# The compare that makes the one-hots of a gate matrix: its row of column numbers read from a PSUM bank

## The reference, cut to what matters

```python
s1, i1 = lax.top_k(s[:, :, 0], P_TOPK)
s2, i2 = lax.top_k(s[:, :, 1], P_TOPK)
cand_i = (i1[..., :, None] * P_NKEYS + i2[..., None, :]).reshape(nt, P_HEADS, P_TOPK * P_TOPK)
top_s, pos = lax.top_k(cand_s, P_TOPK)
idx = jnp.take_along_axis(cand_i, pos, axis=-1)
gate = jax.nn.softmax(top_s, axis=-1)
u = jnp.take(u_tab, idx, axis=0)
act = jax.nn.gelu(jnp.einsum('thkd,td->thk', u, xb), approximate=False) * gate
vv = jnp.take(v_tab, idx, axis=0)
return jnp.einsum('thk,thkd->td', act, vv)
```

## Time and profile before

| | us |
|---|---|
| median of 3 runs | 4235.46 |
| lowest, highest | 4233.41, 4239.32 |
| profiled execution | 4235.86 |
| its span, first to last instruction | 4234.1 |
| busy in the span: PE, DVE, ACT, POOL | 3680.3, 3221.9, 1264.6, 2074.4 |
| gate matrix stage of the first layer, first compare to last evacuation | 1047.0 to 1203.7 |
| of the second layer | 2956.9 to 3113.3 |

### The profile page before, as it was taken

The page is one execution under the profiler, slowest core; times in us unless marked ns, Lnnn a source line. Parts: engine busy times, 40 slices in busy tenths (PEclk is TensorE's granted clock), DMA queues, the critical chain, the costliest instruction groups (busy, mean ns, idle before and its releaser), DMA issues. The chain is left out here.

```text
span 4234.1 us, 51468 instructions
## 1 busy us (share of the span) xinstructions
PE 3680.3 (87%) x17523; PEld 2894.4 (68%) x17523; DVE 3221.9 (76%) x5977; ACT 1264.6 (30%) x2010; POOL 2074.4 (49%) x1349
## 2 busy tenths in 40 slices
PE   6985579896779999999997957894779999999997
PEld 2454355443669989988986546452668998998996
DVE  1036554577979999999998167298979999999998
ACT  1031131111743333333332133101743333333332
POOL 0000000134967767777875000034966777778775
PEclk8987689898989999999998955997989999999999
DMA  4410001341579999999997100111569999999997
GB/s 199 163 43 6 0 1 40 130 170 51 159 233 396 396 398 400 391 405 401 398 397 307 67 23 1 50 40 40 158 221 394 397 398 399 398 401 402 398 396 304
DMA packets 318724, 1013.09 MB, mean 239 GB/s; under 512 B 23351, under 2 KB 121655, under 8 KB 296089
## 3 DMA queue, kind: packets, MB, share of 16 engines
q0 software_dynamic: 149936, 546.03, 33.1%
q1 hardware_dynamic: 166882, 440.55, 27.5%
q10 hardware_dynamic: 1800, 25.24, 1.6%
HBM read 958.16 MB, written 53.56 MB: 239 GB/s over the span
## 5 line engine op out<-in xcount | busy, mean ns | idle before, releaser
L1331 POOL DMA_INDIRECT arena<-in_peer_v,picked x512 | 834.1, 1629 | 238.5 <-issue 122.5
L1331 POOL DMA_INDIRECT arena<-in_peer_u_rows,picked x512 | 765.2, 1495 | 346.5 <-DVE dots L1924 220.4
L831 PE MATMUL pair<-h_hi,u_hi 128*128 128x384 f32 x2048 | 689.5, 337 | 30.9 <-issue 30.9
L831 PE MATMUL pair<-h_lo,u_hi 128*128 128x384 f32 x2048 | 687.5, 336 | 0.0
L831 PE MATMUL pair<-h_hi,u_lo 128*128 128x384 f32 x2048 | 687.2, 336 | 0.0
L1944 DVE SCALAR_TENSOR_TENSOR gate<-arena,act,gate 128x1024 f32<-128x1024 f32 x512 | 640.7, 1279 | 6.7 <-DVE act L1936 6.6
L1924 DVE CUSTOM_DVE_ANT_0 arena<-arena 128x1024 f32<-128x1024 f32 x512 | 612.3, 1219 | 15.1 <-DVE dots L1930 15.1
L831 PEld LDWEIGHTS pair<-h_hi,u_hi 128*128 128x128 f32 x2048 | 387.5, 189 | 40.0 <-issue 34.3
L1108 ACT ACTIVATE u_hi<-ring 128x2048 fp32r<-128x2048 f32 x128 | 245.5, 1919 | 519.5 <-DMA ring<-in_peer_u 519.4
L831 PEld LDWEIGHTS pair<-h_lo,u_hi 128*128 128x128 f32 x2048 | 387.4, 189 | 6.4
L831 PEld LDWEIGHTS pair<-h_hi,u_lo 128*128 128x128 f32 x2048 | 387.1, 189 | 0.0
(11 more groups left out here) (300 smaller groups left out, 5810.5 us busy)
## 6 DMA issues: line engine op xcount, KB each, us to landing
ring<-in_peer_u SPq DMA_DIRECT2D x128, 1024.0 KB, 8.0
ring<-in_peer_v SPq DMA_DIRECT2D x128, 1024.0 KB, 9.3
routing<-arena SPq DMA_DIRECT2D x24, 2048.0 KB, 8.7
arena<-routing SPq DMA_DIRECT2D x64, 768.0 KB, 9.8
ring<-in_w_ada SPq DMA_DIRECT2D x12, 2048.0 KB, 10.2
ring<-in_w_ada ACTq DMA_DIRECT2D x12, 2048.0 KB, 7.8
ring<-in_peer_wq SPq DMA_DIRECT2D x8, 2048.0 KB, 7.9
ring<-in_w_in SPq DMA_DIRECT2D x6, 2048.0 KB, 12.9
```

The lines of the kernel that those rows point to most:

```text
L831: last = mm(pair[:, j, 0:TD], R(u[b][:, P * (KD * j + k):P * (KD * j + k + 1)]), R(h[:, k, :]), start=(k == 0 and i == 0), stop=(k == KD - ...
L1331: pool.indirect_dma_start(gathered[:, b, :], None, rows, bass.IndirectOffsetOnAxis(picked[:, n:n + 1], 0)).then_inc(sem[f"row_in{b}"], 16)
```

## The change

At the beginning of DVE's `routing_matrix` a copy puts the 128 column numbers into the first 128 words of `bank[1]` in PSUM, and waits for its end. The compare of every job reads them from there. Nothing else differs.

```diff
             def routing_matrix(l):
+                link(V.tensor_copy(bank[1][:, 0:P], iota))
                 jobs = TB // 4
...
                             dve.wait_ge(sem["g_full"], i * (2 * jobs) + (hot0 + m + 1))
                             tt(hots[:, m % 4], bc(cols[:, b, 0:2, 4 * n:4 * n + 4], P, 3),
-                               bc(bc(iota, 4, 1), 2, 1), ALU.is_equal).then_inc(sem["hot_ready"], 1)
+                               bc(bc(bank[1][:, 0:P], 4, 1), 2, 1), ALU.is_equal).then_inc(sem["hot_ready"], 1)
```

## The result

| | before | after |
|---|---|---|
| median of 4 runs, us | 4237.14 | 4168.23 |
| lowest, highest | 4233.41, 4239.32 | 4165.0, 4170.4 |
| profiled execution, its span | 4235.9, 4234.1 | 4165.0, 4163.2 |

The changed kernel is faster: the ratio of the times is 0.984, with a 95% interval of 0.9826 to 0.9854. That is 68.9 us by the medians. The lines of the code have moved by one: the copy into the bank is L1879, the column copy L1886, the compare L1893.

A forecast was written before the change was run, and what follows sets the result against it. DVE was taken to bound the routing stage, its compares held up by POOL's multiply. Savings of 32.7 us a layer, 65.4 for two, less 1.7 for clock gaps gave 63.7, so 4171.8 from 4235.5, range 4165 to 4189.

The forecast's parts named there:

- The lockstep and its price: In the middle blocks, DVE's compare and POOL's multiply exclude each other; each compare loses 0.41 us of a 1.55 period.
- The exclusion ends: With one SBUF input left, compares no longer contend with POOL's multiply and follow each other by 1.14 us.
- The PSUM read: Price of reading each compare's second input from PSUM: 0, between -8 and +16 ns.
- twenty middle blocks: Ten middle blocks in each layer fall from 12.46 to 9.48 us, saving 2.98 each, 29.8 a layer.
- the copy: Copying 128x128 into the bank takes 0.3 us a layer, covered by DVE's 2.91 us idle before the fifth compare.
- clock gaps: Two stretches of PE at 1.2 GHz a layer, each losing 1.1 us where one cost 0.66: 1.7 lost altogether.
- the first block: Each layer's first block gains nothing: four compares are hidden, and the next start as PE's slow first jobs free slots.
- What is late next: Limits below DVE's 9.48 us block: ACT's loop through the block turn at 9.2, the DMA to `routing` at 8.98.
- After the stage: Work after the last compare, up to ACT's first dense work, moves along with it and takes no gain back.
- The trimmed case: DMA landings of 9.7 us or 0.06 us per PSUM read make blocks 9.98, time 4182.6; chance 0.20.
- The case of no effect: POOL excludes DVE through the compare's first input or output; period stays 1.55, time 4235.5 plus at most 0.6; chance 0.06.
- The slower case: The compare's repeated PSUM row costs two cycles an element; period 2.21 us, 123 us slower, 4358; chance 0.04.

The follow-up runs named there:

- the version with both edits: Against the changed kernel, POOL copies the columns half a block ahead and ACT's next-block scalings go ahead of the last two evacuations; 4156.1 us.

## Why the prediction came out as it did

The mechanism was right, and the time was 3.6 us below the forecast. The gain itself was 68.9 where 63.7 was forecast, 5.2 more; that the time is off by less is luck, as the median of the kernel before came out 1.6 above the 4235.5 that the forecast counted from. By its own steps:

**The lockstep and its price.** Two engines with one mean, 1556 and 1555, was the sign of it. The 0.41 us that a compare lost was worked out from spacing, without knowing what it was. The kernels with less multiplying show it: the multiply's length less 195 ns, in three doses.
The Trainium skill, SBUF — State Buffer, section "Who interferes with whom", states that DVE and GpSimd share one port pair as an exclusive lock; the trace agrees, in that POOL's multiply of 8 results waits for most of a compare, 1118 ns against 199.

**The exclusion ends.** The compare was forecast near 1.22 and the multiply near 0.62: 1.215 and 0.612. The forecast argued from a replace of another kind, which was thin; moving either input now shows it directly.

**The PSUM read.** Forecast 0, between -8 and +16 ns; measured -3. The prediction's estimate of 65 ns, worked out from the fixed costs in the Trainium skill, VectorE: DVE Perf Modes, section "The TRN2 errata", doesn't hold for this instruction; the trace doesn't show it.

**The sum.** Each term, for both layers together:

| term | forecast, us | measured, us |
|---|---|---|
| twenty middle blocks | 59.6 | 60.7 |
| two last blocks | 5.8 | 5.9 |
| two first blocks, from the fifth compare on | 0 | 1.2 |
| the copy | 0 | 0 |
| clock gaps | -1.7 | in the 60.7: four before, none after |
| sum | 63.7 | 67.8 |

The middle blocks are (124.74 - 94.23) + (124.43 - 94.25) = 60.7. The period is 1.131 and not 1.14; I had it from one pair of compares (2.36 - 1.22), and eight give it more closely. The last block takes from 1155.39 until its last compare is over at 1164.54: 9.15 against 12.08.

**The term that was too small: the first block.** I had argued that PE's slow first jobs set it, so nothing would be gained. In the first layer the next block begins 1061.16 - 1055.86 = 5.30 after the fifth compare, where it took 1061.73 - 1055.40 = 6.33. The slow jobs hide the first four compares but not the last three, which weren't held any more. In the second layer, where the sixth and the seventh compare wait for PE as well (0.49 and 0.43), it is 6.00 where it took 6.20. In both layers that makes 1.03 + 0.20 = 1.2.

**The clock.** I took it that the gaps stay and lose 1.1 us each in place of 0.66. The kernel before does have two in the middle blocks of each layer: over 7 us from 1065, 1126, 2986 and 3085 the clock was granted at 0.76. In the profiled execution of the changed kernel there were none (clock 1.00 in both windows). Its second profile has one, in the second layer: timeline of the block, then the table of windows over the gap.

```profile
2942.07 4.62 DVE L1893 TENSOR_TENSOR arena<-arena,bank 128x1024 f32<-128x1024 f32 x4
2947.54 1.22 DVE L1893 TENSOR_TENSOR arena<-arena,bank 128x1024 f32<-128x1024 f32 x1 [0.85 <-PE pair L819]
2949.24 3.48 DVE L1893 TENSOR_TENSOR arena<-arena,bank 128x1024 f32<-128x1024 f32 x3 [0.49 <-PE pair L819]
...
2953.01 9.14 DVE L1893 TENSOR_TENSOR arena<-arena,bank 128x1024 f32<-128x1024 f32 x8
```

```profile
2943.00:2950.00 7.00, 5.22 (x32) 5.04 (x32) 5.66 (x6) 4.87 (x13) 3.06 (x5) 0.76 0.73 205
```

With the clock granted at 0.76 over 7 us DVE waits twice for PE, and that block takes 2953.01 - 2942.07 = 10.94 in place of 9.42. A gap so costs 1.5 (2.1 in the version with the column copy on POOL), over the 1.1, but in the changed kernel's two profiles it comes once or not at all where before it came twice a layer. Why it comes less often wasn't tried.

The term was also put together wrongly. The 12.46 of a block before is a mean that already holds what the gaps cost there, so gaps that stay would take their whole 1.1 from the saving, 4.4 in all and not 1.7. And the 0.66 was DVE's wait, not the loss: from first compare to first compare that block took 12.9 (1123.76 to 1136.67), its neighbours 12.4, while the block with the gap at 1065 took 12.2 and so lost nothing. That the gaps nearly went away is what kept this from showing, and so it is luck.

**The copy.** 0.29 us, forecast 0.3. It delays the first compare by 0.33, and the fifth waits for PE all the same, with 3.43 of idle time in place of 2.91. From the copy at L1876 to the fifth compare it is 1055.86 - 1046.05 = 9.81, and it was 1055.40 - 1045.59 = 9.81. The cover held.

**What is late next.** ACT's loop was put at 9.2 and measured at 9.25, once DVE was made faster; DVE's own block at 9.48 and measured at 9.42. The order was right, and the room between them 0.17 where 0.3 was forecast. The DMA's share rose to the 0.78 expected, its landings stayed at 8.7. Its floor of 8.98 wasn't put to the test: with the order of ACT for which it was worked out no block was shorter than 9.24, and in the version with both edits, at 9.05, the wait for the write comes later in ACT's order, so that the floor lies lower.

**After the stage.** The last multiply shares its time with a table split (2.60) and the dense work waits 8.93 for the last DMA, both as before. Nothing is taken back: from the copy at L1876 to dense work the first layer saves 34.9 and the second, with 166.7 before and 133.3 after, 33.4. The spans differ by 70.9, 2.5 us more than that. Most of it, 2.3, lies between the first layer's dense work and the second layer's stage, which the change doesn't touch and which takes 1741 to 1745 in the ten profiles; I have no cause for it.

**The rivals.** The trimmed case needed late landings or a price of 0.06 us for the PSUM read, and neither came. The case of no effect falls with the compare's median: neither input excludes DVE by itself, and nor does the output, which goes to SBUF as before. The slower case needed a period of 1.51.

## What to carry to other kernels

When two engines at work on different data show the same mean time for different work, and each is much shorter where it runs alone, look for what they exclude each other over, and price it by shrinking one of the two. A constant operand that is read again and again is the cheapest thing to move: one copy of 0.29 us per layer ended it here, and which of the two inputs was moved made no difference to the compare. Once the bound engine has room, look for the next loop before trimming more; here two edits, neither of which showed in the times by itself, together gave 8 us by the profiles and 13 by the medians.

## What the runs showed of the hardware

- **The loss is not symmetrical.** A compare of 1.215 us beside a multiply lost only the multiply's length less 195 ns, and nothing (3 ns) beside the shortest. The multiply lost much more: the one of 8 results took 1118 ns in place of 199. A short instruction on POOL costs DVE nothing here and itself some 0.92 us, three quarters of a compare.
- **POOL's multiply:** 199, 392 and 608 ns at the shortest for 8, 128 and 256 results, some 1.65 ns for each further result.
- **A blocked instruction is shown as busy.** POOL's busy time fell by 166 us with no work removed, which is what hid its idle time in the profile before.
